# A third gate_up program and experts in an order made on the chip, in a hybrid decoder layer

## The chip, the cores and the metric

One NeuronCore of a Trainium2 chip runs the whole layer in one launch. The metric is the device time of one execution in microseconds (us). The kernel before has a median of 2191.45 us over 3 runs (2190.69 to 2195.38). The profiled execution took 2190.32 us.

## The reference

```python
# one layer: x (1, 1024, 1024) float32, 1024 tokens t of width D = 1024
h = rmsnorm(x)
p = h @ w_in                      # D x 3584: ret_q|ret_k|ret_v|ret_gate|sb_q|sb_k|sb_v
A = swish_gate(rmsnorm(retention(rotary(q), rotary(k), v)))   # 4 heads x 128
B = stick_breaking(rmsnorm(q), rmsnorm(k), v)                 # 8 heads x 64, strictly causal
x = x + concat(A, B) @ w_out
xn = rmsnorm(x)
top4 of xn @ w_router + b_router over 32 experts, softmax over the four
for each expert e, its tokens:
    gu = xn @ w_gate_up[e] + b_gate_up[e]          # 1024 x 2048, gate and up interleaved
    hidden = (clip(up) + 1) * min(gate, 7) * sigmoid(1.702 * gate)
    y = hidden @ w_down[e] + b_down[e]             # 1024 x 1024
x = x + sum over the four experts of weight * y
```

All inputs and the output are float32. How many tokens an expert gets is known on the chip only; 4096 pairs fall on 32 experts.

## The kernel before, in words

**Projection** (`project`, L946 and L953, until some 385 us). The product with `w_in` runs in two halves of 512 tokens. Operands are split in an upper part (rounded to fp32r) and a lower one (the rest), and three products add up: `products`. Tokens come to feature-major form by `turn_tile`: ScalarE takes sums of squares, VectorE inverts, and `x_norm` is made for tile 0 and 1 on one engine and for tiles 2 and 3 on POOL (L592), which then makes `w_lo[0]` (L594). `upper_tokens` (ScalarE) and `lower_tokens` (VectorE, L1337) split the tokens; for the second half both stand at group `NG // 2`, when the last group of the first half has left. Retention steps and the head norms are woven between the groups.

**Stick-breaking attention** (`scores`, `turn_rest`, `values`; some 385 to 508 us). `values` (L1069) multiplies by `dv`, differences of neighbouring rows of v. SyncE copies v shifted by one row into `dv` in two parts and POOL subtracts (L613), all of it after the last projection group.

**Output projection and router** (L1103 to L1133, until some 620 us). Each token tile goes through `out_proj`, `turn`, `route` and `route_sum` on TensorE, `residual`, `scaled`, `inverse_norm` and `best` (the four best logits) on VectorE; `route_sum` and `best` trail three tiles behind. `keep_busy` issues transposes nobody reads.

**Lists and tables** (some 620 to 647 us). Counts and ranks come from products with triangular ones (`f_rank`). `first_hot` and `token_list` make the index list of expert 0, POOL gathers its rows by indirect DMA, `turn_main` and `turn_over` transpose them. VectorE's `tables()` (L1620 to L1632) then makes what later experts need: three bf16 parts of each token's weight (`twx`) and the places of each token (`f_n`). It stands before block 0, and the engines' waits for it end just ahead of the first gate_up.

**The 32 expert blocks** (647 to some 2171 us). Each engine has a loop over the experts in their own order, n = 0 to 31: `block_pe` on TensorE, `block_dve` on VectorE, `block_act` on ScalarE, `load_expert` on SyncE. A block holds up to CAP = 168 tokens; further ones would go to a second loop of `more` blocks, which here runs zero times. In a block:

- TensorE loads the expert's count from `it_i` into a register (L1277) and chooses one of two gate_up programs by it (L1284): 140 tokens wide, or 168. Each has its own instructions. `gate_up` takes 8 steps f, each two parts of 8 matmuls with 128x128 float32 weights out of `gu_ring` (every second column) and `xT` as what moves (L1246). A float32 matmul is two instructions. After f = 3 `token_list` (24 small matmuls, L1162) makes the list of the next expert.
- `down` takes 48 matmuls of 512 columns (L1226), with the transposes of the next expert's tokens (L1169, L1175) in the middle, and for tokens over 128 64 narrow matmuls for each 32 rows (L1234, `down_over`), under a branch each.
- VectorE in each step f empties the bank (L1739, L1741), makes the hidden values (L1747, L1749) and their lower part (L1728), splits down weights (`lower`, L1723) and, after f = 1, compares positions for the next list (`list_hot`, L1644). The banks alternate, so TensorE's step f needs VectorE's emptying of step f - 2. In block 0 `table_part(f)` adds small operations for the table of further blocks.
- SyncE reloads `gu_ring` in four chunks of 2 MB and `dn_ring` in two as they come free.

The choice of the program, in block_pe:

```python
tokens = e.value_load(it_i[0:1, 1, bass.ds(n, 1)], min_val=-S, max_val=S)
...
    with e.If(tokens <= widths[half - 1]):
        choose(widths[:half])
    with e.Else():
        choose(widths[half:])
```

Of the kernel before, what the change touches and what calls it, by code (L numbers as in the profile page):

```python
# [60 lines left out]
WIDTHS = (140, CAP)  # L61
IT_STEPS = 17
F_SPREAD = 20
# [55 lines left out]
def layer(nc, x, attn_norm_g, w_in, ret_norm_g, sb_q_norm_g, sb_k_norm_g, w_out, ffn_norm_g,  # L119
          w_router, b_router, w_gate_up, b_gate_up, w_down, b_down, consts, rope, out):  # L120
    with ExitStack() as ctx:
# [81 lines left out]
        dv = region(ring, 3072, NT, CH)  # L203
# [44 lines left out]
        a_norm_p = sem("a_norm_p")  # L248
# [55 lines left out]
        e_norm = sem("e_norm")  # L304
        e_st = [sem(f"e_st{i}") for i in range(2)]
# [10 lines left out]
        it_step = sem("it_step")  # L316
        l_wrap = sem("l_wrap")
# [170 lines left out]
        f_w0 = region(work, 1576, NT, 4)  # L488
        f_t0 = region(work, 1608, NT)
        f_cnt = region(mix, 7744, NE)  # L490
        f_over = region(mix, 7776, NE)
# [4 lines left out]
        b_rows = region(work, 4096, 2048)[0:NE]  # L496
# [3 lines left out]
        dn_ring = region(ring, 16384, KD, D)  # L500

# [13 lines left out]
        def wait_norm(e, i):  # L515
            if 2 <= i < HT:
                e.wait_ge(a_norm_p, i - 1)
            else:
                e.wait_ge(a_norm, i + 1 if i < 2 else i - 1)

        @block.sync
        def _(sp_eng):
# [25 lines left out]
            for q in range(2):  # L548
                lo, n = HT * q, HT - 1 + q
                for r0, r1 in ((1, 113), (113, P)):  # L550
                    e.dma_start(dv[r0:r1, lo:lo + HT], sv[r0 - 1:r1 - 1, lo:lo + HT]).then_inc(z_shift[q], 16)
                e.dma_start(dv[0:1, lo + 1 - q:lo + HT], sv[P - 1:P, lo - q:lo + HT - 1]).then_inc(z_shift[q], 16)
# [3 lines left out]
            for c in range(2):  # L556
                e.dma_start(dn_ring[:, :, c * 512:(c + 1) * 512], dn_r[0, c]).then_inc(dn_in[c], 16)
            for i in range(NT):
                e.wait_ge(e_x2, 2 * i + 2)
                e.dma_start(outr[i], x2[:, i % 2]).then_inc(e_st[i % 2], 16)  # L560
                e.wait_ge(e_norm, i + 1)
                e.dma_start(xnr[i], xn2[:, i % 2]).then_inc(e_st[i % 2], 16)
            e.wait_ge(e_prj, 2 * NT)
            for c in range(4):
# [3 lines left out]
                e.dma_start(gu_ring[:, :, c * 512:(c + 1) * 512], gu_r[0, c]).then_inc(gu_in[c], 16)  # L568

# [8 lines left out]
            with e.Fori(1, NE) as n:  # L578
                load_expert(n, n)
# [8 lines left out]
        def _(e):  # L588
            for i in range(2, HT):
                e.wait_ge(a_inv, i + 1)  # L590
                e.wait_ge(a_tr, 2 * i - 2)
                e.tensor_scalar(x_norm[i % 2], x_in[i % HT], rstd[:, i:i + 1], None, ALU.mult).then_inc(a_norm_p, 1)  # L592
# [3 lines left out]
            e.dma_start(wr, w_router[0].rearrange("(k p) n -> p k n", p=P)).then_inc(rt_in, 16)  # L596
            for th in range(2):
                for q in range(2 * RH):
                    dst = (rqT if q < RH else rkT)[:, q % RH, :]
                    e.wait_ge(prj_free, freed(NG // 2 * th + q + 1))  # L600
                    e.tensor_tensor(dst, dst, prj_tmp[:, q % 2], ALU.add).then_inc(rope_ok, 1)
                for c in range(HT * th, HT * (th + 1)):
# [6 lines left out]
            e.memset(dv[0:1, 0], 0.0).then_inc(z_zero, 1)  # L609
            e.wait_ge(z_zero, 1)  # L610
            for i in range(NT):
                e.wait_ge(z_shift[i // HT], 48)
                e.tensor_tensor(dv[:, i], sv[:, i], dv[:, i], ALU.subtract).then_inc(z_dv, 1)  # L613
# [15 lines left out]
            e.wait_ge(e_st[1], 128)  # L629
# [8 lines left out]
            e.wait_ge(g_xT, 4)  # L638
# [40 lines left out]
        def _(e):  # L679
# [25 lines left out]
            def upper_tokens(th):  # L705
                e.wait_ge(a_hx, NT * (th + 1))
                if th:
                    e.wait_ge(prj, NG // 2)
                for k in range(0, KD, 2):
# [8 lines left out]
            root(HT - 1)  # L718
            upper_slab(0)
            upper_tokens(0)  # L720
            for g, u in enumerate(groups):
                th, c = u["th"], u["c"]
                if g == NG // 2:
                    upper_tokens(1)
# [27 lines left out]
                if g in SPLIT:  # L752
                    upper_slab(SPLIT[g])
                if g in NORM:
# [72 lines left out]
            for i in range(NT):  # L827
# [7 lines left out]
                e.activation(e_dump, x2[:, i % 2], ACT.Square, accum_out=ssq2[:, i:i + 1]).then_inc(e_sq, 1)  # L835
                e.wait_ge(e_ms, i + 1)
# [5 lines left out]
            for i in range(NT - 3, NT):  # L842
# [3 lines left out]

            e.wait_ge(e_log, NT)
            e.wait_ge(e_st[0], 128)
            e.wait_ge(e_st[1], 128)
            e.dma_start(b_rows, b_gate_up[0]).then_inc(bias_in, 16)  # L850
# [6 lines left out]
            e.wait_ge(sc_done, 48)  # L857
            e.wait_ge(f_step, F_SPREAD)
            e.activation(bias_d, b_raw, ACT.Copy).then_inc(b_cast, 1)
            for g in range(1, 3):  # L860
                e.wait_ge(b_sub, g)
                for h in range(g, 3):
                    rows = slice(h * NE, (h + 1) * NE)
                    cp = e.activation(bias_d[rows], b_raw[rows], ACT.Copy)
                cp.then_inc(b_cast, 1)
# [19 lines left out]
            def block_act(n):  # L885
                for f in range(KD):
# [8 lines left out]
                    e.activation(hid_hi[:, f], hid[:, f, 0:P], ACT.Copy).then_inc(h_hi, 1)  # L895
                for q in range(5, 8):
# [911 lines left out]
```

## Time and profile before

| | |
|---|---|
| median of 3 runs | 2191.45 us (2190.69 to 2195.38) |
| profiled execution | 2190.32 us, span 2188.0 us |
| mean granted TensorE clock | 0.988 |
| TensorE matmuls busy | 2126.4 us, 97% of the span |
| TensorE weight loads busy | 1891.9 us, 86% (beside the matmuls) |
| VectorE | 1271.9 us, 58% |
| ScalarE | 765.9 us, 35% |
| GpSimd (POOL) | 346.5 us, 16% |
| DMA | 509.53 MB, mean 233 GB/s |
| the chain that ended last | PE 95%, DVE 2%, issue 1%, DMA 1% |

The span runs from the first to the last instruction; the execution's own time has 2.3 us around it. PE is TensorE's matmuls, PEld its weight loads, DVE VectorE, ACT ScalarE, SP SyncE; a q behind an engine is its sequencer. "issue" is time in which an engine waited for nothing that the profile shows. A clock of 1.00 is the full 2.4 GHz, 0.5 the lower level. The chain names at each moment what the end of the run hung on, so its shares, not the busy times, say where time can be taken out.

### The profile page before, as it was taken

Reading aid. Unit: us, or ns where it says so; the run is one execution under the profiler, and the core shown is the slowest. Engines: PE = TensorE matmul, PEld = TensorE weight load, DVE = VectorE, ACT = ScalarE, POOL = GpSimd, SP = SyncE. Lnnn points to the kernel's source line nnn. Section 1 sums busy time; section 2 is a strip of 40 time slices with the busy share of each in tenths; the row PEclk is TensorE's granted clock in tenths of the full one; section 3 lists DMA queues with packets and bytes.
Section 4 is the critical chain, followed back from the end, with each engine's and each line's share of the span. In section 5 each row is a group of like instructions: output and inputs, shape, how many; then the busy total and the mean of one; then the engine's idle time right before and its main releaser. Section 6 shows DMA issues by size and latency. Waiting matters only on the chain.

```text
span 2188.0 us, 41248 instructions
## 1 busy us (share of the span) xinstructions
PE 2126.4 (97%) x16059; PEld 1891.9 (86%) x16060; DVE 1271.9 (58%) x2564; ACT 765.9 (35%) x1369; POOL 346.5 (16%) x243
## 2 busy tenths in 40 slices
PE   7999999899979999999999999999999999999996
PEld 6887888677868999898899999899999999999996
DVE  6434534886466665456556655555666655666654
ACT  4143133666222333233333323333333332333332
POOL 3100200200011111111121111111212111212121
PEclk9999999999979999999999999999999999999998
DMA  5321221304366988788789888877998887999883
GB/s 179 105 79 58 97 96 39 116 1 154 126 209 220 323 307 293 238 279 307 274 298 318 306 293 280 307 270 263 320 325 307 306 294 264 319 327 331 309 290 89
DMA packets 253683, 509.53 MB, mean 233 GB/s; under 512 B 7466, under 2 KB 36318, under 8 KB 253342
## 3 DMA queue, kind: packets, MB, share of 16 engines
q1 hardware_dynamic: 230124, 451.95, 57.9%
q0 software_dynamic: 21968, 51.67, 9.6%
q10 hardware_dynamic: 1536, 5.15, 0.7%
q8 instruction: 38, 0.62, 0.1%
q14 instruction: 17, 0.14, 0.0%
HBM read 473.09 MB, written 33.55 MB: 232 GB/s over the span
## 4 chain that ended last, share of the span: by engine, by line
PE 95%; DVE 2%; issue 1%; DMA 1%; POOL 0%; ACT 0%; ACTq 0%; SPq 0%; DVEq 0%; POOLq 0%
PE bank L1246 46%; PE bank L1226 16%; PE bank L946 10%; PE bank L953 4%; PE bank L1234 3%; PE bank L1056 2%; PE bank L1069 2%; PE bank L1103 1%; PE bank L1169 1%; PE bank L1105 1%; PE bank L1104 1%; PE bank L1162 1%; PE bank L1040 1%; PE bank L1175 1%; PE bank L1211 1%
## 5 line engine op out<-in xcount | busy, mean ns | idle before, releaser
L1246 PE MATMUL bank<-hx,ring 128*128 128x140 f32 (+1 forms) x8192 | 1021.9, 287 | 7.5 <-DVEq L1684 7.5
L1246 PEld LDWEIGHTS bank<-hx,ring 128*128 128x128 f32 x8192 | 1015.1, 197 | 10.3 <-DVEq L1684 7.7
L1226 PE MATMUL bank<-work_r,hx_r 128*128 128x512 f32 x1024 | 335.0, 408 | 0.0
L1723 DVE TENSOR_TENSOR mix_r<-ring,work_r 128x1024 fp32r<-128x1024 f32 x256 | 305.0, 1223 | 41.1 <-ACT work_r L872 40.9
L889 ACT ACTIVATE hx<-hx 128x168 f32<-128x168 f32 x256 | 88.0, 344 | 595.8 <-DVE hx L1739 593.4
L1739 DVE TENSOR_SCALAR hx<-bank,small 128x168 f32<-128x168 f32 x256 | 100.3, 392 | 298.7 <-PE bank L1246 289.3
L872 ACT ACTIVATE work_r<-ring 128x1024 fp32r<-128x1024 f32 x256 | 257.7, 1042 | 0.0
L1226 PEld LDWEIGHTS bank<-work_r,hx_r 128*128 128x128 f32 x1024 | 188.1, 189 | 43.9 <-issue 10.4
L1226 PE MATMUL bank<-mix_r,hx_r 128*128 128x512 f32 x512 | 200.0, 391 | 0.0
L649 POOL DMA_INDIRECT out_x<-hx,small x32 | 52.0, 1625 | 659.7 <-ACT hx L882 621.3
L880 ACT ACTIVATE hx<-bank,small 128x512 f32<-128x512 f32 x64 | 44.0, 688 | 313.9 <-PE bank L1175 167.3
L616 POOL DMA_INDIRECT hx<-xn_scratch,small x33 | 33.9, 1028 | 574.1 <-issue 568.1
L895 ACT ACTIVATE hx_r<-hx 128x128 fp32r<-128x128 f32 x256 | 78.8, 308 | 109.0 <-DVE hx L1749 109.0
L946 PE MATMUL bank<-hx_r,mix_r 128*128 128x512 f32 x480 | 112.5, 392 | 3.6 <-DVE hx_r L1337 3.6
L1226 PEld LDWEIGHTS bank<-mix_r,hx_r 128*128 128x128 f32 x512 | 96.1, 188 | 21.0
L946 PE MATMUL bank<-hx_r,work_r 128*128 128x512 f32 x480 | 113.7, 394 | 0.0
L946 PEld LDWEIGHTS bank<-hx_r,mix_r 128*128 128x128 f32 x480 | 89.6, 188 | 23.5 <-issue 5.2
L1644 DVE TENSOR_TENSOR work<-hx,cst 128x3072 bf16<-128x3072 f32 x32 | 107.2, 3351 | 0.0
L946 PEld LDWEIGHTS bank<-hx_r,work_r 128*128 128x128 f32 x480 | 89.7, 188 | 20.2 <-issue 1.9
L652 POOL DMA_INDIRECT out_x<-hx,small x64 | 100.7, 1573 | 19.5 <-issue 19.5
L1741 DVE TENSOR_SCALAR hx<-bank,small 128x168 f32<-128x168 f32 x256 | 98.0, 383 | 0.0
L1658 DVE TENSOR_TENSOR hx<-bank,small 128x512 f32<-128x512 f32 x66 | 42.6, 686 | 86.0 <-PE bank L1169 86.0
(244 smaller groups left out, 2318.4 us busy)
## 6 DMA issues: line engine op xcount, KB each, us to landing
ring<-in_w_gate_up SPq DMA_DIRECT2D x128, 2048.0 KB, 11.0
ring<-in_w_down SPq DMA_DIRECT2D x64, 2048.0 KB, 17.5
mix<-in_w_in SPq DMA_DIRECT2D x14, 1024.0 KB, 5.0
work<-in_w_in SPq DMA_DIRECT2D x14, 1024.0 KB, 5.1
ring<-in_x SPq DMA_DIRECT2D x8, 512.0 KB, 6.3
hx<-in_w_out SPq DMA_DIRECT2D x1, 4096.0 KB, 14.0
work<-in_x ACTq DMA_DIRECT2D x8, 512.0 KB, 4.7
out_x<-work SPq DMA_DIRECT2D x8, 512.0 KB, 4.5
```

The source lines that it names most:

```text
L652: e.indirect_dma_start(out=out_quarters, in_=y_o[:, r], in_offset=None, compute_op=ALU.add, out_offset=bass.IndirectOffsetOnAxis(ap=idx_sc ...
L872: e.activation(dn_hi[:, nh, k:k + 2], dn_ring[:, k:k + 2, nh * CH:(nh + 1) * CH], ACT.Copy).then_inc(c_hi, 1)
L889: e.activation(sg[:, f % 2], g1[:, f % 2], ACT.Sigmoid, scale=GALPHA).then_inc(m_sig, 1)
L895: e.activation(hid_hi[:, f], hid[:, f, 0:P], ACT.Copy).then_inc(h_hi, 1)
L946: mm = e.matmul(dst, ws[b][:, k, u["s"] * P:(u["s"] + 1) * P], xs[:, k, :], start=k == 0 and (xs is x_hi and ws is w_hi), stop=k == KD - 1 ...
L953: mm = e.matmul(dst, xs[:, KD // 2 * b + k, u["s"] * P:(u["s"] + 1) * P], ws[b].rearrange("p (k a) n -> p k (a n)", a=2)[:, k, :], start=b ...
L1226: mm = e.matmul(bank[2 + t][:, :], h[:, k], w[:, t, k], start=False, stop=k == KD - 1 and w is dn_lo, skip_group_check=True)
L1246: mm = e.matmul(bank[f % 2][:, part * CAP:part * CAP + w], gu_ring[:, k, f * 256 + part:(f + 1) * 256:2], xT[:, k, 0:w], start=k == 0, sto ...
L1644: e.tensor_tensor(hot, pos_s.unsqueeze(2).to_broadcast([P, NT, NH * P]), slot_at.unsqueeze(1).to_broadcast([P, NT, NH * P]), ALU.is_equal) ...
L1723: e.tensor_tensor(dn_lo[:, nh, k:k + 2], dn_ring[:, k:k + 2, nh * CH:(nh + 1) * CH], dn_hi[:, nh, k:k + 2].bitcast(F32), ALU.subtract).the ...
L1739: e.tensor_scalar(g1[:, b], bank[b][:, 0:CAP], be[:, f:f + 1], GLIM, ALU.add, ALU.min)\
L1741: e.tensor_scalar(u1[:, b], bank[b][:, CAP:2 * CAP], be[:, 8 + f:9 + f], GLIM + 1.0, ALU.add, ALU.min).then_inc(m_up, 1)
```

## The change

- `WIDTHS` has three widths, 128, 140 and 168, so `block_pe` has three gate_up programs, in this order in the code, and down behind them. The second loop (`more`) has the three as well.
- Blocks 0, 1 and 2 stay experts 0, 1 and 2 (`FIXED`). While block 1 runs, VectorE's `order_part` gives every later expert a key (its class by count: to 128, to 140, over; then its number), ranks the keys by 32x32 comparisons, and writes experts and counts in that order into `it_i`. `it_go` then opens blocks 3 to 31 for TensorE and SyncE. SyncE and VectorE load each block's expert from `it_i`.
- `tables()` no longer stands before block 0. `second_lists` (expert 1's list alone) and `weight_table`, `second_hot`, `place_table` run on VectorE inside block 0, `table_part` in block 2. The bias parts of POOL and ScalarE go into block 0.
- Openings: at the start `x_norm` of tile 2 is made on ScalarE and of tile 3 on VectorE, with 14 filler transposes ahead of the first tile; half of the second half's token splits come three groups earlier; the first four tiles of `dv` are shifted and subtracted during the projection; 20 filler transposes stand before the output projection; `route_sum` and `best` of the first tiles come earlier, and the last normalised tile is stored from ScalarE's queue; `b_gate_up` is loaded early into a part of `dn_ring`, whose second half is loaded later; the bias transposes come right behind the counts.

The diff, cut (a "..." marks what is left out):

```diff
-WIDTHS = (140, CAP)
-IT_STEPS = 17
-F_SPREAD = 20
+WIDTHS = (128, 140, CAP)
+LATER = (128, 140)
+FIXED = 3
+IT_STEPS = 29
+F_SPREAD = 21
...
+            def shifted(q):
+                lo = HT * q
+                for r0, r1 in ((1, 113), (113, P)):
+                    e.dma_start(dv[q][r0:r1], sv[r0 - 1:r1 - 1, lo:lo + HT]).then_inc(z_shift[q], 16)
+                e.dma_start(dv[q][0:1, 1 - q:HT], sv[P - 1:P, lo - q:lo + HT - 1]).then_inc(z_shift[q], 16)
...
+                if j == NSLAB // 2 + 4:
+                    e.wait_ge(prj_free, freed(NG // 2))
+                    e.wait_ge(xs_lo, KD)
+                    shifted(0)
...
-            for c in range(2):
-                e.dma_start(dn_ring[:, :, c * 512:(c + 1) * 512], dn_r[0, c]).then_inc(dn_in[c], 16)
+            e.dma_start(dn_ring[:, :, 0:512], dn_r[0, 0]).then_inc(dn_in[0], 16)
+            e.dma_start(b_rows, b_gate_up[0].rearrange("e (a n) -> e a n", n=512)).then_inc(bias_in, 16)
...
+            e.wait_ge(bias_tr, 1)
+            e.dma_start(dn_ring[:, :, 512:1024], dn_r[0, 1]).then_inc(dn_in[1], 16)
...
             with e.Fori(1, NE) as n:
-                load_expert(n, n)
+                e.wait_ge(it_go, n + 1)
+                load_expert(n, e.value_load(it_i[0:1, 0, bass.ds(n, 1)], min_val=0, max_val=NE - 1))
...
-            for i in range(2, HT):
-                e.wait_ge(a_inv, i + 1)
-                e.wait_ge(a_tr, 2 * i - 2)
-                e.tensor_scalar(x_norm[i % 2], x_in[i % HT], rstd[:, i:i + 1], None, ALU.mult).then_inc(a_norm_p, 1)
...
+            e.activation(x_norm[0], x_in[2], ACT.Copy, scale=rstd[:, 2:3]).then_inc(a_norm_2, 1)
...
+                if g == NG // 2 - 3:
+                    upper_tokens(1, 0, KD // 2)
...
+                if i == NT - 1:
+                    logits_part(NT - 3)
...
+            e.dma_start(xnr[NT - 1], xn2[:, (NT - 1) % 2]).then_inc(e_last, 16)
...
             e.wait_ge(const_in, 16)
+            keep_busy(14, bank[2])
...
+            keep_busy(20, bank[4])
...
+                    if nh and i >= 3:
+                        route_sum(i - 3)
...
-            keep_busy(10, bank[4])
+
+            e.wait_ge(bias_in, 16)
+            e.wait_ge(e_x2, 16)
+            for j in range(16):
+                mm = e.transpose(bank[j // 8][:, (j % 8) * NE:(j % 8 + 1) * NE],
+                                 b_rows[:, j % 8 // 2, j % 2 * 256 + j // 8:j % 2 * 256 + 256:2], cst[0:NE, C_ID:C_ID + NE])
+            mm.then_inc(bias_tr, 1)
...
-            keep_busy(8, bank[3])
+            keep_busy(4, bank[3])
...
             with e.Fori(0, NE) as n:
+                e.wait_ge(it_go, n + 1)
                 block_pe(n)
...
+            to_raw(0)
+            normalise(3)
+            for i in range(1, HT):
...
+                if 3 <= i < NT:
+                    best(i - 3)
...
+            def second_lists():
+                step(e.tensor_scalar(pos_t, tok_id, f_cnt[:, 1:2], None, ALU.add))
+                step(e.scalar_tensor_tensor(pos_t, rank[:, :, 1], -2.0, pos_t, ALU.mult, ALU.add))
+                step(e.tensor_tensor(pos_t, pos_t, f_n[:, :, 1], ALU.mult))
+                step(e.tensor_tensor(pos_s, rank[:, :, 1], pos_t, ALU.add))
+                step(weight_parts(1))
+                step(e.tensor_reduce(f_t, f_b.rearrange("p i k e -> p i e k"), X, ALU.add))
+
+            def second_hot():
+                e.tensor_tensor(hot, pos_s.unsqueeze(2).to_broadcast([P, NT, NH * P]),
+                                slot_at.unsqueeze(1).to_broadcast([P, NT, NH * P]), ALU.is_equal).then_inc(l_hot, 1)
+                e.sem_inc(l_wrap, 1)
+                e.sem_inc(l_pos, 1)
+
+            def weight_table():
                 step(e.tensor_copy(twx[:, :, 0:NE, 0], f_t))
                 step(e.tensor_tensor(f_t, f_t, twx[:, :, 0:NE, 0], ALU.subtract))
                 step(e.tensor_copy(twx[:, :, 0:NE, 1], f_t))
                 step(e.tensor_tensor(f_t, f_t, twx[:, :, 0:NE, 1], ALU.subtract))
                 step(e.tensor_copy(twx[:, :, 0:NE, 2], f_t))
                 step(e.memset(twx[:, :, NE, :], 0.0))
+
+            def place_table():
+                e.memset(it_base, 0.0)
+                e.memset(it_low, 0.0)
...
-            tables()
...
+            def order_part(f):
+                if f == 0:
+                    table(e.tensor_copy(c_f, it_i[:, 1, 0:NE]))
+                    table(e.tensor_scalar(c_class, c_f, float(LATER[0]), None, ALU.is_gt))
+                    for w in LATER[1:]:
+                        table(e.scalar_tensor_tensor(c_class, c_f, float(w), c_class, ALU.is_gt, ALU.add))
+                    table(e.scalar_tensor_tensor(c_class, iota_e, float(FIXED), c_class, ALU.is_ge, ALU.mult))
+                    table(e.scalar_tensor_tensor(c_key, c_class, float(NE), iota_e, ALU.mult, ALU.add))
+                elif f == 2:
+                    table(e.tensor_tensor(c_less, c_key.unsqueeze(2).to_broadcast(square),
+                                          c_key.unsqueeze(1).to_broadcast(square), ALU.is_gt))
+                    table(e.tensor_reduce(c_rank, c_less, X, ALU.add))
+                elif f == 3:
+                    table(e.tensor_tensor(c_at, iota_e.unsqueeze(2).to_broadcast(square),
+                                          c_rank.unsqueeze(1).to_broadcast(square), ALU.is_equal))
+                elif f == 4:
+                    table(e.tensor_tensor(c_less, c_at, iota_e.unsqueeze(1).to_broadcast(square), ALU.mult))
+                    table(e.tensor_reduce(it_f[:, 0, 0:NE], c_less, X, ALU.add))
+                elif f == 5:
+                    table(e.tensor_tensor(c_less, c_at, c_f.unsqueeze(1).to_broadcast(square), ALU.mult))
+                elif f == 6:
+                    table(e.tensor_reduce(it_f[:, 1, 0:NE], c_less, X, ALU.add))
+                    table(e.tensor_copy(it_i[:, :, FIXED:NE], it_f[:, :, FIXED:NE]))
+                    e.sem_inc(it_go, NE - FIXED)
...
-                    if f == 1:
+                    if f == 1 and opening:
+                        second_hot()
+                    elif f == 1:
                         e.wait_ge(l_sum, n + 1)
                         if x_next is None:
-                            x_next = e.value_load(it_i[0:1, 0, bass.ds(n + 1, 1)], min_val=0, max_val=NE)
+                            x_next = e.value_load(it_i[0:1, 0, n + 1:n + 2] if isinstance(n, int) else
+                                                  it_i[0:1, 0, bass.ds(n + 1, 1)], min_val=0, max_val=NE)
                         list_hot(n + 1, x_next)
-                    if opening:
+                    if opening and f == 0:
+                        weight_table()
+                    if opening and f == 2:
+                        place_table()
+                    if ordering:
+                        order_part(f)
+                    if tabling:
                         table_part(f)
...
-            block_dve(0, 0, 1, True)
-            assert built[0] == IT_STEPS
-            with e.Fori(1, NE - 1) as n:
-                block_dve(n, n, n + 1)
-            block_dve(NE - 1, NE - 1)
+            block_dve(0, 0, 1, opening=True)
+            block_dve(1, 1, 2, ordering=True)
+            block_dve(2, 2, tabling=True)
+            assert built[0] == IT_STEPS, built[0]
+            with e.Fori(FIXED, NE) as n:
+                block_dve(n, e.value_load(it_i[0:1, 0, bass.ds(n, 1)], min_val=0, max_val=NE - 1))
```

TensorE, the expert loop. Before, the block's register load, the 140 program and the start of the 168 program, as the instructions stand (`bank<-hx,ring` are the gate_up products):

```order
L1277 TENSOR_LOAD hx
L1277 ISA x2
L1284 COMPARE_AND_BRANCH
L1239 ISA
L1242 ISA
L1243 ISA
L1246 MATMUL bank<-hx,ring 128x140 x16
...
L1284 UNCONDITIONAL_BRANCH
L1239 ISA
L1242 ISA
L1243 ISA
L1246 MATMUL bank<-hx,ring 128x168 x16
```

After, the same place: the first branch leads over the 128 program to a second one.

```order
L1313 TENSOR_LOAD hx
L1313 ISA x2
L1320 COMPARE_AND_BRANCH
...
L1282 MATMUL bank<-hx,ring 128x128 x16
...
L1320 UNCONDITIONAL_BRANCH
L1320 COMPARE_AND_BRANCH
...
L1282 MATMUL bank<-hx,ring 128x140 x16
...
L1320 UNCONDITIONAL_BRANCH
...
L1282 MATMUL bank<-hx,ring 128x168 x16
...
L1322 UNCONDITIONAL_BRANCH
L1247 MATMUL bank<-cst,small 128x512
```

Each program holds 128 such matmuls and the 24 of `token_list`; `down` begins at L1247, behind all three.

VectorE, block 1 after the change (emptying a bank is L1830, the list L1709, the sort L1785 to L1802):

```order
L1709 TENSOR_TENSOR work<-hx,cst 128x3072
L1830 TENSOR_SCALAR hx<-bank,small 128x168
L1832 TENSOR_SCALAR hx<-bank,small 128x168
L1817 TENSOR_TENSOR hx_r<-hx,hx_r 128x128
L1838 TENSOR_TENSOR hx<-hx 128x168
L1840 SCALAR_TENSOR_TENSOR hx<-hx 128x168
L1792 TENSOR_TENSOR mix<-small 128x1024
L1794 TENSOR_REDUCE small<-mix 128x32
...
L1796 TENSOR_TENSOR mix<-cst,small 128x1024
L1812 TENSOR_TENSOR mix_r<-ring,work_r 128x1024 x2
```

The operations of the sort (over 1024 elements each) stand between the steps, ahead of the next emptying.

## Rows read from the trace of the kernel before

**Rows 1.** The page's chain that ended last, shares of the span by line.

```profile
PE bank L1246 46%; PE bank L1226 16%; PE bank L946 10%; PE bank L953 4%; PE bank L1234 3%; PE bank L1056 2%; PE bank L1069 2%; PE bank L1103 1%; PE bank L1169 1%; PE bank L1105 1%; PE bank L1104 1%; PE bank L1162 1%; PE bank L1040 1%; PE bank L1175 1%; PE bank L1211 1%
```

**Rows 2.** Chain by time (start us, us, what); 841: a 168-wide block, 1573: at most 128 tokens.

```profile
841.27 18.24 PE bank L1246 x128
...
1573.57 15.26 PE bank L1246 x128
...
1618.01 7.03 PE bank L1246 x59
```

**Rows 3.** Groups by form: xcount | busy us, mean ns | idle before <-releaser, whole run.

```profile
L1246 PE MATMUL bank<-hx,ring 128*128 128x140 f32 x6912 | 837.4, 283 | 7.5 <-DVEq L1684 7.5
...
L1246 PE MATMUL bank<-hx,ring 128*128 128x168 f32 x1280 | 184.5, 306 | 0.0
...
L1234 PE MATMUL bank<-ring,hx 128*32 128x256 f32 x1216 | 68.8, 379 | 0.0
```

**Rows 4.** Timeline of TensorE, 140 to 144 us: start us, us, operation.

```profile
140.37 1.05 PE L985 MATMUL bank<-ring,work 128*128 128x128 f32 x8
...
142.16 1.06 PE L1004 MATMUL bank<-ring 128*128 128x128 f32 x8
```

**Rows 5.** Windows: us, busy us (x) of PE, PEld, DVE, ACT, POOL, PEclk, DMA share, GB/s.

```profile
1573.57:1588.83 15.26, 15.26 (x135) 15.24 (x135) 8.59 (x20) 4.66 (x10) 4.78 (x3) 1.00 0.95 282
1589.41:1604.77 15.36, 15.36 (x130) 15.34 (x130) 12.35 (x30) 6.85 (x13) 3.63 (x3) 1.00 1.05 393
392.80:399.70 6.90, 6.05 (x31) 4.34 (x32) 3.15 (x3) 1.49 (x5) 6.90 (x6) 0.51 0.91 316
```

**Rows 6.** Chain by time, block 0.

```profile
647.24 17.93 PE bank L1246 x128
...
665.75 15.37 PE bank L1246 x128
681.12 2.79 issue
```

**Rows 7.** Branches of L1284 (all; after 700 us) and L1298: xcount: ns min/median/max.

```profile
L1284 PEldq COMPARE_BRANCH  x59: 76/169/4927, 638.0 to 2155.8; - x59
...
L1284 PEldq COMPARE_BRANCH  x57: 76/169/209, 700.2 to 2155.8; - x57
...
L1298 PEldq COMPARE_BRANCH  x1: 3287/3287/3287, 2169.2 to 2169.2; - x1
```

**Rows 8.** VectorE operation on 1024 elements: xcount: ns min/median/max, first and last start.

```profile
L1612 DVE TENSOR_TENSOR work<-cst,work x1: 1226/1226/1226, 631.0 to 631.0; 128x1024 f32<-128x1024 bf16 x1
```

**Rows 9.** The index load L1277 of two blocks, and those blocks' first matmuls in the chain.

```profile
L1277 PEldq TENSOR_LOAD <-hx x1: 303/303/303, 1042.4 to 1042.4; - x1
1044.89 15.26 PE bank L1246 x128
...
L1277 PEldq TENSOR_LOAD <-hx x1: 303/303/303, 1279.5 to 1279.5; - x1
1281.03 1.99 PE bank L1246 x14
```

**Rows 10.** Waits around the openings (us in total, times, longest), and POOL's group L592.

```profile
PE bank L946 <- DVE hx_r L1337: 2.6, 1, 2.6
...
PE bank L1069 <- POOL ring L613: 4.1, 1, 4.1
...
PE bank L1103 <- DVE hx_r L1548: 3.4, 1, 3.4
...
L592 POOL TENSOR_SCALAR ring<-ring,small 128x1024 f32<-128x1024 f32 x2 | 5.7, 2842 | 10.4 <-PE bank L918 10.4
```

**Rows 11.** DMA queues, 675 to 705 us and 740 to 2160 us: packets, MB, share.

```profile
q8 instruction: 5, 0.08, 1.1%
...
q1 hardware_dynamic: 183383, 369.78, 72.6%
q0 software_dynamic: 20160, 47.20, 13.5%
```

More of the change, by code:

```diff
@@ L316, in layer @@
         it_step = sem("it_step")
+        it_go = sem("it_go")
         l_wrap = sem("l_wrap")
@@ L596, in _, with differences @@
             e.dma_start(wr, w_router[0].rearrange("(k p) n -> p k n", p=P)).then_inc(rt_in, 16)
+            def differences(q):
+                for i in range(HT):
+                    e.wait_ge(z_shift[q], 48)
+                    e.tensor_tensor(dv[q][:, i], sv[:, HT * q + i], dv[q][:, i], ALU.subtract).then_inc(z_dv, 1)
             for th in range(2):
@@ L608, in _ @@
             e.wait_ge(prj_free, freed(NG))
[L609 to L613, printed above, removed]
+            differences(1)
             def gather_main(landed):
@@ L703, in upper_slab, with upper_tokens @@
                 e.activation(w_hi[j % 2], w_raw[j % 2], ACT.Copy).then_inc(ws_hi, 1)
-            def upper_tokens(th):
+            def upper_tokens(th, first, last):
                 e.wait_ge(a_hx, NT * (th + 1))
                 if th:
-                    e.wait_ge(prj, NG // 2)
-                for k in range(0, KD, 2):
+                    e.wait_ge(prj, end_of[NSLAB // 2 - 2] if first == 0 else NG // 2)
+                for k in range(first, last, 2):
                     e.activation(x_hi[:, k:k + 2], x_raw[:, k:k + 2], ACT.Copy).then_inc(xs_hi, 1)
@@ L855, in _, with bias_part @@
                 .then_inc(bias_ok, 1)
[L857 to L865, printed above, removed]
+            def bias_part(g):
+                if g == 0:
+                    e.wait_ge(sc_done, 48)
+                    e.wait_ge(f_step, F_SPREAD)
+                    e.activation(bias_d, b_raw, ACT.Copy).then_inc(b_cast, 1)
+                else:
+                    e.wait_ge(b_sub, g)
+                    for h in range(g, 3):
+                        rows = slice(h * NE, (h + 1) * NE)
+                        cp = e.activation(bias_d[rows], b_raw[rows], ACT.Copy)
+                    cp.then_inc(b_cast, 1)
             def upper(n, q):
@@ L1089, in _, with route_sum @@
             e.wait_ge(rt_in, 32)
+            def route_sum(i):
+                e.wait_ge(e_pev, i + 1)
+                if i:
+                    e.wait_ge(e_logb, 6 * i - 5)
+                e.matmul(bank[7][:, 0:NE], l_part[:, i % 2], cst[:, C_SEL:C_SEL + NE], start=True, stop=True).then_inc(e_log, 1)
             def out_proj(i):
@@ L1127, in route @@
                 mm.then_inc(e_part, 1)
-            def route_sum(i):
-                e.wait_ge(e_pev, i + 1)
-                if i:
-                    e.wait_ge(e_logb, 6 * i - 5)
-                e.matmul(bank[7][:, 0:NE], l_part[:, i % 2], cst[:, C_SEL:C_SEL + NE], start=True, stop=True).then_inc(e_log, 1)
             for i in range(NT + 3):
@@ L1189, in _ @@
             mm.then_inc(p_list, 1)
-            e.wait_ge(bias_in, 16)
-            e.wait_ge(e_x2, 16)
-            for j in range(16):
-                mm = e.transpose(bank[j // 8][:, (j % 8) * NE:(j % 8 + 1) * NE],
-                                 b_rows[:, (j % 8) * 256 + j // 8:(j % 8) * 256 + 256:2], cst[0:NE, C_ID:C_ID + NE])
-            mm.then_inc(bias_tr, 1)
+            keep_busy(10, bank[4])
             e.wait_ge(l_hot, 1)
@@ L1332, in lower_slab, with lower_tokens @@
                 e.tensor_tensor(w_lo[j % 2], w_raw[j % 2], w_hi[j % 2].bitcast(F32), ALU.subtract).then_inc(ws_lo, 1)
-            def lower_tokens(th):
-                for q in range(KD // 2):
+            def lower_tokens(th, first, last):
+                for q in range(first // 2, last // 2):
                     e.wait_ge(xs_hi, KD // 2 * th + q + 1)
```

112 lines of the change are left out of this document (63 added, 49 removed).

## The prediction

> **What bounds the kernel now.** I read the chain of waits first. TensorE carries it: the gate_up line L1246 alone is 46% of the span and the down line L1226 16% [rows 1]. So a term counts only where TensorE gets shorter work or stops waiting, and a wait on any other engine costs nothing until TensorE stands for it. The chain inside an expert block of the loop (the stretch of an expert with at most 128 tokens) has no gap: 15.26 us for 128 instructions of L1246, TensorE busy for all of the other half's 15.36 [rows 5], and the next block's first matmul 44.44 us after this one's [rows 2]. The groups by form give 6912 instructions at a moving width of 140 and 1280 at 168, 256 to a block: 27 and 5 blocks [rows 3]. L1234, the rows over 128, ran 1216 times at 64 for up to 32 rows: 19 pieces [rows 3]; one block has two of them, so 18 experts hold over 128 tokens, 5 of them over 140, and **14 hold at most 128**. Those 14 are computed 140 wide today.
>
> **The 128-wide program.** 128 instructions take 15.26 us at width 140 and 18.24 at 168 [rows 2], so 119.2 and 142.5 ns each: 0.83 ns per column and 2.5 ns besides. At 128 columns this gives 109.2. The weight load of 128 columns runs beside each matmul and may set a floor. Other f32 matmuls with 128 columns show one: 16 of them, eight each of L985 and L992, start between 140.37 and 142.16 us, 111.9 ns each [rows 4]. L1246 reads its weights with a stride of two, which rows 4 do not test, so its floor may lie anywhere up to the 119.2 it runs at. Per block of 256 the gain is 256 x (119.2 - 109.2) = 2.6 us at best, 1.9 at 111.9, 1.1 halfway from there to no gain (115.0), 0 at 119.2. I take 1.9: it is the nearest row, and at 140 and 168 one line per column still fits with 2.5 ns over. 14 x 1.9 = **-27** (-36 to -15, and 0 as a rival).
>
> Do the weights arrive in time? In this half block the DMA engines are 0.95 busy [rows 5]. That is the one resource near its limit, and a shorter block pulls 12 MB through 42.5 us instead of 44.4. If it saturates, the loss is a part of the 27 and not a cost beyond it: I count nothing. VectorE works 8.59 us in the first half and 12.35 in the second [rows 5]; two halves of 14.3 still hold that.
>
> **The tables.** `tables()` stands between the last token copies and the first gate_up; L1246's only idle time is 7.5 us behind it [rows 3]. It moves to block 0, where VectorE waits for TensorE's slow first steps. The first half of block 0 took 17.93 us against 15.37 for its second [rows 6]: the clock had fallen to its lower level (1.2 GHz) in the wait, and a shorter wait may give back 1 of these 2.6. -7.5 - 1. What takes it back: block 0 is expert 0, of the 140 class (its half takes 15.37 and a piece of L1234 follows), so it must now jump over the 128 program, and a jump over a program that has not run is dear. The one in block 0 today took 4927 ns, and TensorE stood 2.79 us for it [rows 6, 7]. The new one comes at the entry, where little is queued: **+3** (0 to 5). The old exit jump stays as it is. Sum **-5.5** (-9 to -2).
>
> **The sort.** `order_part` adds, in block 1, six compare, multiply or reduce steps over 32x32 = 1024 elements with one more reduce, 1.23 us each by L1612's operation of that size [rows 8], so some 8.6 us, of which 8.4 fall in steps 2 to 6. The gate_up part of a block holds 20.9 us of VectorE work [rows 5], steps 1 to 6 some 19.2 of it, since step 0 has only a step's 1.7; with the sort 27.6. In the time from the end of its step 1 to that of step 6 TensorE has five steps of 3.6 us and the token list, 18.6, and VectorE may be one to two steps late (5.4 in the middle) before a PSUM bank is missing. 27.6 - 18.6 - 5.4 = 3.6, and the last hidden parts reach the down product about 1 us late: **+4.5** (0 to +8). Block 2's `table_part` is what block 0 has today, without a stall: 0. The waits on `it_go` in TensorE's and SyncE's streams hold the loop only at block 3; SyncE's queue behind it has the weight loads of expert 3, which can't start before the ring is free anyway, late in block 2's gate_up: 0. The index load per block on VectorE and SyncE is a register load of about 0.3 us (TensorE's own takes that [rows 9]), and VectorE is busy only 8.59 of the first half's 15.26 us: 0.
>
> **The openings.** Each shortens one wait, and each is bounded by it. At the start, two normalisations leave POOL (2842 ns each, with w_lo0 queued behind [rows 10]) for ScalarE and VectorE: -4 (0 to -5). At the half boundary TensorE waited 2.6 us for x_lo; half of it is now made before: -2. At the attention's start it waited 4.1 us for POOL's differences [rows 10], behind a DMA that now runs during the projection for the first four tiles: -4, and the lower clock in the 6.9 us after it (0.51 [rows 5]) should partly go: -2. At out_proj keep_busy can only keep the clock, the 3.4 us wait [rows 10] stays: -1.7. Router tail: one `best` and two logits less behind the last tile: -1.6. Bias transposes moved off the chain and four fewer filler transposes: -2.5. Sum -17.8; each moved step meets the next late thing (SyncE's queue now waits for x_lo before w_in slabs; the last xn store sits on ScalarE's queue), so I give a fifth back: **-14** (-20 to -6).
>
> **Switches of class.** Sorted, the classes run 140, 128, 140, then 128, 140, 168 in blocks: four jumps into a program that lies elsewhere, at 0 to 4 us each: **+3** (0 to +17). Here the classes' own new code is fetched.
>
> Sum: -27 - 5.5 + 4.5 - 14 + 3 = **-39** against the profiled execution's 2190.3, so 2151.3; the median of the runs shown is 1.1 us above that execution, so **2152**. Own range 2137 to 2172.
>
> **Rival 1, slower: the loop no longer stays loaded.** Today instructions arrive by their own DMA queue: 5 packets of 16 KB between 675 and 705 us, and from 740 to 2160 us none at all [rows 11]. So the whole loop stays loaded. Counted in the program, one turn of the loop is some 1,560 TensorE instructions (512 matmuls and weight loads in each gate_up program, 48 of the token list), with the third program about 2,130; at 64 bytes each 6.1 packets become 8.3. The trace shows the seven packets held over which today's loop lies, and says nothing of a ninth. If eight are held, the loop's last piece pushes out its first, and the jump back misses once per block. A miss is 3287 ns (L1298, idle queues) to 4927 (L1284, full ones) [rows 7]. The index load leads the block's first matmul by 2.5 us (1042.4 to 1044.89) and after a block with rows over 128 by 1.5 [rows 9]; some 1 us of it is register and branch work, so 1.5 and 0.5 are cover. 14 x (1.8 to 3.4) + 17 x (2.8 to 4.4) = 73 to 123 us, less 39: **2225 to 2275**. It decides from the point where the loop exceeds what is held. Sorting does not help the jump back. For it: the 4927 ns jump, and 16 KB packets fetched only once the code is near. Against: no jump after 700 us took over 209 ns [rows 7], so nothing is dropped as long as it fits.
>
> The Trainium skill ("Runtime: NRT & Kernel Launch", section "Instruction fetch mechanics") gives TensorE room for 2048 instructions, refilled 256 at a time, and makes a taken branch outside the window wait for its page; by that figure this rival holds. The same section speaks of a window of two pages, by which today's loop would stall every block, and the trace shows that it doesn't.
>
> **Rival 2: the weight load is the floor.** If L1246 can't go below 119 ns, the 27 are gone and the rest stays: -12, **2179**. The 111.9 ns of rows 4 speaks against it.
>
> **Rival 3: the change does not do what it says**, as the sort comes too late or in the old order: then TensorE waits on `it_go` at block 3 once, at most 5 us, and the classes are mixed. With the loop resident this is 2157, inside the first case.
>
> **How the numbers follow.** A measurement of this kernel tells about 0.2% (4.4 us) from no change. The first case with rival 3: 0.57. Rival 1: 0.38. Rival 2: 0.05. Faster 0.59 (the first case and most of the second rival), slower 0.37, same 0.04, where a cheap rival 1 meets the gains. The range must reach from 2137 into the middle of rival 1: 2137 to 2262.
>
> **What would show it.** In the profile after: L1246 at form 128x128 x3584 with halves near 14.3 us; the chain without gaps at the block borders; no packets of the instruction queue from 800 us on. One packet or more per block there, and an "issue" gap of 2 to 4 us before each block's first L1246, prove rival 1. The gap before the first L1246 should be near 0, block 1 should hold 3 to 6 us of waits on VectorE, and the waits of rows 10 should be gone save that at out_proj. If the blocks of 128 shrink by under 1 us, rival 2 holds.

## The result, and the profile after

The changed kernel takes **2581.3 us** (median of 4 runs, 2578.2 to 2584.5); beside it the kernel before took 2192.1. The ratio is 1.177 (95% interval 1.175 to 1.180): 389 us slower, where 39 us faster were forecast, and far above the range. The page of the kernel after begins (busy us, share of the span, instructions), with its instruction queue, the chain by engine and the gate_up group:

```profile
PE 2202.0 (85%) x16089; PEld 1946.5 (76%) x16090; DVE 1281.5 (50%) x2583; ACT 726.9 (28%) x1339; POOL 343.2 (13%) x241
...
q8 instruction: 210, 3.44, 0.6%
...
PE 79%; issue 11%; DVE 6%; ACT 1%; DMA 1%; ACTq 0%; POOL 0%; DVEq 0%; POOLq 0%
...
L1282 PE MATMUL bank<-hx,ring 128*128 128x128 f32 (+2 forms) x8192 | 1055.6, 293 | 211.7 <-issue 210.3
```

TensorE has about as much to do as before, but it stands 210 us on "issue" just ahead of gate_up matmuls, that is, it waits for nothing that the profile shows. The queue that brings instructions moved 210 packets of 16 KB, where before it moved 38. In the DMA view, which answers to [rows 11], the queues are, for 862 to 1388 us (twelve blocks of the 128 class) and for 1527 to 1600 us (one block of the 140 class):

```profile
q1 hardware_dynamic: 74873, 150.99, 79.7%
q0 software_dynamic: 8064, 18.88, 14.6%
...
q8 instruction: 10, 0.16, 0.9%
```

There is no instruction packet at all in the twelve blocks, and there are ten in one block of the next class. The branches of TensorE agree, since a dear branch (one of over 1 us) stands only where packets come; the lines are L1320 (the choice of the program) and L1330 (the jump back), first for 860 to 1380 us, then for one block of the 140 class and the edges of its neighbours (count: ns min/median/max):

```profile
L1320 PEldq COMPARE_BRANCH  x23: 76/169/169, 889.2 to 1374.3; - x23
L1330 PEldq COMPARE_BRANCH  x11: 207/208/208, 901.9 to 1342.9; - x11
...
L1320 PEldq COMPARE_BRANCH  x3: 81/6326/7522, 1527.6 to 1567.8; - x3
L1330 PEldq COMPARE_BRANCH  x2: 4051/4074/4096, 1522.6 to 1595.9; - x2
```

In the first stretch no branch is dear, though the loop is one of 2,130 instructions there too and each block jumps over two programs. In the second the jump over the 128 program takes 7.5 us, the jump over the 168 program 6.3 and the jump back 4.1. In the chain by time (start us, us, what) that block reads:

```profile
1524.51 11.16 issue
1535.67 18.49 PE bank L1282 x128
...
1554.75 15.38 PE bank L1282 x128
...
1576.57 3.23 issue
1579.80 7.01 PE bank L1262 x24
...
1597.87 10.45 issue
```

The windows of its parts (columns as in [rows 5]) show what the gaps cost besides:

```profile
1524.50:1535.70 11.20, 0.04 (x2) 0.04 (x1) 0.33 (x2) 1.42 (x3) 4.78 (x3) 0.66 0.89 258
1535.67:1554.16 18.49, 18.49 (x135) 18.47 (x136) 8.28 (x18) 1.65 (x5) 0.00 (x0) 0.83 0.69 231
1554.75:1570.13 15.38, 15.37 (x128) 15.16 (x128) 12.34 (x30) 6.84 (x13) 3.71 (x3) 1.00 0.79 283
1570.13:1579.80 9.67, 0.61 (x1) 0.39 (x2) 5.34 (x9) 3.49 (x5) 0.00 (x0) 0.62 0.82 287
```

From one block's gap to the next are 73.4 us, where such a block took 47.9: 11.2 us of gap ahead of gate_up, 9.7 ahead of down, 3.2 in the first half, whose mean granted clock is 0.83 after 0.66 in the gap (18.49 us against 15.26 in [rows 2]), and 1.5 in the first down products (7.01 us in the chain against 5.47 without a gap). Over the 11 sorted blocks of this class that is 281 us, over the five of the 168 class about 100, over blocks 0 and 2 another 28.

The groups by form answer to [rows 3]. Behind them stands the chain: the entry of block 0, the first matmuls of blocks 1 and 2, and the second halves of two blocks of the 128 class:

```profile
L1282 PE MATMUL bank<-hx,ring 128*128 128x128 f32 x3584 | 431.1, 283 | 8.4 <-issue 7.2 <-DVE hx L1832 1.2
L1282 PE MATMUL bank<-hx,ring 128*128 128x140 f32 x3328 | 428.7, 294 | 113.3 <-issue 113.0 <-DVE hx L1832 0.2
L1282 PE MATMUL bank<-hx,ring 128*128 128x168 f32 x1280 | 195.9, 318 | 90.0 <-issue 90.0
```

```profile
627.63 1.97 PE bank L1210 x8
...
631.81 5.61 issue
637.42 9.47 PE bank L1282 x64
...
702.41 9.19 PE bank L1282 x64
...
750.29 7.64 PE bank L1282 x64
...
876.33 15.18 PE bank L1282 x128
...
920.43 15.18 PE bank L1282 x128
```

The 14 blocks are 128 wide as intended, but half a block takes 15.18 us against 15.37, and the block 44.10 against 44.44.

### The profile page after: what moved, and what is told of

It reads as the page before. It is cut to its first block, busy times and chain, and to the rows that moved or that the text cites. A ratio compares the mean times of both kernels' runs of the same rounds, so it can differ in the third digit from the quotient of the medians.

```text
span 2576.3 us, 41675 instructions
## 1 busy us (share of the span) xinstructions
PE 2202.0 (85%) x16089; PEld 1946.5 (76%) x16090; DVE 1281.5 (50%) x2583; ACT 726.9 (28%) x1339; POOL 343.2 (13%) x241
## 4 chain that ended last, share of the span: by engine, by line
PE 79%; issue 11%; DVE 6%; ACT 1%; DMA 1%; ACTq 0%; POOL 0%; DVEq 0%; POOLq 0%
PE bank L1282 38%; PE bank L1262 15%; PE bank L978 8%; PE bank L985 3%; PE bank L1270 3%; DVE mix_r L1812 2%; PE bank L1088 1%; PE bank L1101 1%; PE bank L1144 1%; PE bank L1210 1%; PE bank L1146 1%; PE bank L1145 1%; ACT work_r L900 1%; PE bank L1203 1%; PE bank L1072 1%
## 5 line engine op out<-in xcount | busy, mean ns | idle before, releaser
L1282 PE MATMUL bank<-hx,ring 128*128 128x128 f32 (+2 forms) x8192 | 1055.6, 293 | 211.7 <-issue 210.3
L1282 PEld LDWEIGHTS bank<-hx,ring 128*128 128x128 f32 x8192 | 1045.4, 202 | 220.9 <-issue 217.9
L1262 PE MATMUL bank<-work_r,hx_r 128*128 128x512 f32 x1024 | 355.8, 430 | 69.2 <-issue 63.5
L1830 DVE TENSOR_SCALAR hx<-bank,small 128x168 f32<-128x168 f32 x256 | 100.2, 391 | 516.4 <-PE bank L1282 502.1
L1262 PEld LDWEIGHTS bank<-work_r,hx_r 128*128 128x128 f32 x1024 | 202.7, 203 | 120.5 <-issue 80.4
L1262 PE MATMUL bank<-mix_r,hx_r 128*128 128x512 f32 x512 | 211.0, 412 | 0.0
L1262 PEld LDWEIGHTS bank<-mix_r,hx_r 128*128 128x128 f32 x512 | 103.4, 202 | 24.4
L1709 DVE TENSOR_TENSOR work<-hx,cst 128x3072 bf16<-128x3072 f32 x31 | 103.9, 3352 | 0.0
```

Source lines behind the costliest of these rows:

```text
L1262: mm = e.matmul(bank[2 + t][:, :], h[:, k], w[:, t, k], start=False, stop=k == KD - 1 and w is dn_lo, skip_group_check=True)
L1282: mm = e.matmul(bank[f % 2][:, part * CAP:part * CAP + w], gu_ring[:, k, f * 256 + part:(f + 1) * 256:2], xT[:, k, 0:w], start=k == 0, sto ...
L1709: e.tensor_tensor(hot, pos_s.unsqueeze(2).to_broadcast([P, NT, NH * P]), slot_at.unsqueeze(1).to_broadcast([P, NT, NH * P]), ALU.is_equal) ...
L1830: e.tensor_scalar(g1[:, b], bank[b][:, 0:CAP], be[:, f:f + 1], GLIM, ALU.add, ALU.min)\
```

## The theory, and a count made with it

**Theory 1.** TensorE's instructions lie in pieces of 256 (16 KB). Eight are held; a landing in a piece also calls the next one; the one brought or used longest ago goes first. A block touches, in the order of the code, the head of the loop, its own gate_up program and down, with one piece ahead behind each. For the 128 class these are eight pieces: head and program adjoin (four, with the one ahead), then down (four). For the 140 class, whose program lies in the middle, they are ten; for the 168 class too, as it lands at the second branch behind the 128 program on its way. Eight pieces just fit. Ten pieces in turn through eight places means that each is gone when it is wanted.

These rules make a small count (the pieces' positions from the fetches of the two traces), which says how many fetches and dear branches each block has. For the changed kernel it gives 0 where one block of the 128 class follows another, 10 where blocks of the other two follow each other, 51 dear branches in all; the trace has 0, 140 packets in the 14 such blocks between the first and the last of that stretch, and 51 (without the one behind the loop). As the positions come from this trace, the agreement is a fit; the runs below are the test.

My first count had seven pieces for the 128 class, and the expectation of e1 says so. The packets show eight. In the DMA view, block 3 (128 class, behind one of 140; 810.4 to 857.7 us) has the first line, and block 16 (140 class, behind one of 128; 1387.5 to 1448.5 us) the second:

```profile
q8 instruction: 4, 0.07, 0.6%
...
q8 instruction: 6, 0.10, 0.7%
```

With seven pieces they would be 3 and 7; with eight they are the 4 and 6 that came.

**Rivals:** the sort, its index loads and waits; any loop over 2048 instructions; the length of the way that is jumped over.

## The experiments

**e1, the 128 program alone taken out.**

```diff
-WIDTHS = (128, 140, CAP)
-LATER = (128, 140)
+WIDTHS = (140, CAP)
+LATER = (140,)
-IT_STEPS = 29
+IT_STEPS = 28
```

> The changed kernel without its 128-wide program (classes to 140 and over; the sort, the moved tables and the openings stay). Theory 1 (TensorE holds eight pieces of 256 instructions, each jump or step also calls the next one, the oldest goes first; a block of the 140 or 168 class touches nine or ten of the three-program loop, one of the 128 class seven): the loop of 1,565 instructions lies in seven pieces and one ahead, nothing is fetched after block 1, no branch over 0.4 us after it, time 2192 less some 7 for the openings, 8 for the tables, plus 4 for the sort, = 2178 to 2184. Rival (the sort, the index loads or the wait on it_go make the blocks long): over 2400, with blocks of the 140 class near 74 us.

2175.4 us (2175.2 to 2177.7), ratio 0.992 (0.990 to 0.994). 38 packets, as before, on its page:

```profile
q8 instruction: 38, 0.62, 0.1%
```

Everything else of the change is in this kernel, so in this setting the 389 us and 17 more are the third program's. Without it, the sort, the index loads and the wait on it_go cost next to nothing.

**e2, and without the sort** (order_part reduced to the copy of the counts and the opening of it_go).

> As the run before, and the experts stay in their own order (order_part only copies the counts and opens it_go). Theory 1: no fetches in the loop either, block 1 shorter by the 3.8 us that it is longer than the other blocks of its class in the changed kernel: 2174 to 2180. If sorting gives something back through fewer changes of program, it is not faster than the sorted one.

2176.8 us (2173.6 to 2181.2), ratio 0.993 (0.991 to 0.995). Block 1 is shorter (44.56 us against 46.40 in e1), though by 1.8 and not by 3.8 us, and the two kernels' times can't be told apart: the sort is nearly free, and with two programs buys nothing.

**e3, the choice turned.** The 168 class jumps from the loop's head.

```diff
-                    half = len(widths) // 2
+                    half = (len(widths) + 1) // 2
```

> The changed kernel with the choice turned: the first branch asks for 140, so a block of the 168 class jumps from the head of the loop straight to its program and no longer lands at a second branch behind the 128 program. Theory 1: the 168 class now touches seven or eight pieces (28, 29, 33 to 37 in my count) and stays loaded: its blocks fall from 74 us to 54 (fetches from 10 a block to 0, after the first), the 140 class stays at 73 to 74 with 10 fetches: 2581 less 80 to 100 = 2480 to 2500. Rival (any loop over 2048 instructions misses once the far part is used; or the gap of 18 us is the length of the way jumped over, some 3.7 us per piece): the 168 class stays at 74 us, 2581.

2484.7 us (ratio 1.133), 97 less than the changed kernel. The chain has the halves of two blocks of the 168 class without a gap between blocks, 53.90 us from one to the next:

```profile
2253.34 18.24 PE bank L1282 x128
2272.17 18.35 PE bank L1282 x128
2307.24 18.24 PE bank L1282 x128
```

The first block of the 168 class fetches two pieces, the other four none. The blocks of the 140 class stay at 72 to 75 us with 10 fetches each. The loop is as long as before, the way jumped over too; only one landing on the way is gone. That refutes both the bare length and the distance.

**e4, three programs in the kernel before, experts in their own order.**

```diff
-WIDTHS = (140, CAP)
+WIDTHS = (128, 140, CAP)
```

> The kernel before with WIDTHS (128, 140, 168) and nothing else: three programs, the experts' own order. Theory 1: a block that follows one of the same class can find its pieces only if the class is the 128 one; my count gives some 47 dear branches (51 in the changed kernel) at about 7.9 us each (2581 less 2177, over 51): 2192 + 371 less 5 = 2540 to 2570. Rival (the sort is what costs): near 2190.

2493.2 us (ratio 1.137). The count of dear branches was right: 47 in the loop (214 packets in all), none where a 128 block follows another, one at a change into or out of that class, three in a 140 or 168 block behind one of those two. The fetches are 0, 4 to 6 and 9 to 11, where the count with eight pieces has 0, 4 to 6 and 9 or 10. My price was too high (2493 less 2187 over 47 is 6.5 us instead of 7.9). The sorted kernel has about as many dear branches (51) and is still 88 us slower than this one; e9 asks where that comes from.

**e5 and e6, code that never runs.** The two-program kernel of e2, with transposes under a branch that is never taken at the start of down, 128 of them in e5 and 64 in e6:

```diff
             def down(n, tokens):
+                with e.If(tokens > S - 1):
+                    keep_busy(128, bank[4])
```

> The two-program kernel in the experts' own order (e2_two_natural, 2177 us), with 128 filler transposes (256 instructions) at the start of the down part under a branch that is never taken: they never run, and the loop has 1,821 instructions, under 2048. Theory 1: what counts are pieces of 256, with the one called ahead at each landing; in my count every block now touches nine pieces where eight are held: 8 or 9 fetches and 2 dear branches in nearly every block, 286 fetches in all, each block 15 to 20 us longer: 2177 + 31 x 18 = 2650 to 2800. (If the loop's head lies a quarter of a piece later than I think, only the five blocks of the 168 class and their followers: 51 fetches, some 2220.) Rival (2048 instructions of any alignment are held): 2177 to 2190, 38 or 39 fetches.

2728.5 us (ratio 1.244), 318 packets, 9 in nearly every block (my count had 8 and 9 by turns, 286 in all), 90 dear branches in the loop, nearly three a block where I had counted two (why the third one is dear stays open):

```profile
q8 instruction: 318, 5.21, 0.9%
```

> The same with 64 filler transposes (128 instructions). Theory 1: eight pieces still hold a block of either class: no fetches after block 1, 2177 to 2185 (one more branch per block, some 0.2 us of sequencer time that lies behind queued work). Rival (the branch or filler itself costs): as far above 2177 as the run before in half measure.

2180.2 us (ratio 0.994), 38 packets. A loop of 1,821 instructions is refetched in every block and one of 1,693 is not, though the 128 more never run. This fits a limit of eight pieces, the called-ahead ones among them, and not one of 2048 instructions of any position.

**e7, the stride of the weights.** The kernel before with widths 128 and 168, and gate_up's weights read as neighbouring columns, so that gate and up are computed from other columns than the reference's:

```diff
-WIDTHS = (140, CAP)
+WIDTHS = (128, CAP)
-                                          gu_ring[:, k, f * 256 + part:(f + 1) * 256:2], xT[:, k, 0:w],
+                                          gu_ring[:, k, f * 256 + part * P:f * 256 + (part + 1) * P], xT[:, k, 0:w],
```

> The kernel before with widths 128 and 168, and the gate_up weights read as 128 neighbouring columns instead of every second one (other columns are multiplied, so gate and up hold other features; the amount of work is the same). Of 128 instructions at width 128, half a block: 15.18 us in the changed kernel (118.6 ns each). Theory A (the stride of the weight load sets that floor): 14.2 to 14.4 us, 111 to 112.5 ns, as L985 to L1004 run, and the load's record falls from 196 to 191 ns. Rival B (a floor of its own for these f32 passes, or of VectorE's steps): 15.1 to 15.2 as before.

2240.6 us in its one run, as 18 experts are now computed 168 wide. Half a block at width 128 in its chain, and all its weight loads by form:

```profile
721.53 14.40 PE bank L1246 x128
```

```profile
L1246 PEld LDWEIGHTS bank<-hx,ring 128*128 128x128 f32 x8192 | 1064.1, 191 | 10.6 <-DVEq L1684 7.7
```

112.5 ns each instead of 118.6, with the same weights brought in. The stride sets the floor, and it holds 1.6 of the 1.9 us a block that I had counted on.

**e8, the tables back before block 0** (second_lists, weight_table and place_table called there, not in block 0), the rest as e2.

> e2_two_natural with the list, weight and place tables made again before block 0 instead of inside it. Theory 1 (the wait of 7.5 us before the first gate_up is real time and block 0 hides the tables): 2177 + 6 to 9 = 2183 to 2186. Rival (block 0 pays for them with waits on VectorE): 2177 within 2.

2183.5 us (2183.2 to 2187.0), ratio 0.996 (0.995 to 0.998). The old wait is back, as the page shows:

```profile
L1282 PE MATMUL bank<-hx,ring 128*128 128x140 f32 (+1 forms) x8192 | 1021.9, 287 | 8.4 <-DVEq L1751 8.0
```

So moving the tables gives 6.7 us. The rest, this kernel against the one before, is 9.3: the openings, less 2 us that block 2 now takes longer (49.9 us against 47.9), since `table_part` stands in it.

**e9, the loop a quarter of a piece further on**, the changed kernel with 40 filler transposes in place of 8 behind turn_over.

> The changed kernel with 32 more filler transposes (64 instructions, 3.5 us if they are not covered) in TensorE's stream ahead of the loop, so that the whole loop lies a quarter of a piece further on. Theory 1 with the pieces where I place them: today the jump out of the 140 program lands on the last few instructions of a piece (34.97 of 35), so two pieces must come one after the other before down can run, and TensorE stands 9.7 us there; with the shift it lands at 35.2, one piece is enough, 9 fetches instead of 10 in a block of the 140 class, and the block falls from 73.5 to about 68.5 (where the three-program kernel in its own order has them); the 128 class stays without fetches at 44.1. Eleven blocks: 2581 - 55 + 3 = 2520 to 2540. Rival (the pieces do not matter, only the length): 2581 to 2585.

2507.0 us (ratio 1.143), 74 less than the changed kernel, and 13 below what I expected. In the DMA view a block of the 140 class has nine packets:

```profile
q8 instruction: 9, 0.15, 1.0%
```

Its chain ahead of down:

```profile
1544.26 4.35 issue
1548.61 0.61 PE bank L1247
1549.22 7.47 PE bank L1262 x24
```

The gap ahead of down is 4.4 us instead of 9.7, the block 66 to 67 us instead of 73.4. The same program with the same jumps thus loses or saves 74 us by where its loop begins. The gap ahead of down fits a landing on the last instructions of a piece, which has to wait for two pieces. In e4, whose loop begins elsewhere, that gap is 4.5 us too (at 1252.85), so this accounts for most of the 88 us between the changed kernel and e4. Four more dear branches at 6.5 us would be another 26, an estimate; against that stand the 16 us that e4 lacks of the tables and openings.

## Why the prediction was wrong

**The step that failed** is the one that the sum took for granted: that the loop stays loaded, which I gave 0.57. The rows spoke neither way beyond seven packets, and I let the better story (a gain in each term) have the larger half. I had the right rival, with the right number of places, and **mis-stepped in its mechanics**: "the jump back misses once per block" and "Sorting does not help the jump back". A block of the 128 class behind another misses never, one of the other two in a row of such blocks at all three of its jumps. What counts is how many pieces one block touches, with those called ahead, and not whether the loop's end pushes out its head. The rival's 73 to 123 us came out near 400 (281, 100 and 28), partly by that number and partly because I priced a miss by its branch alone. Right behind one dear jump, the next took 6.5 to 7.6 us, as the piece called ahead by the first was still on its way (the order of the packets suggests this, no run tests it), and the half block behind each such gap ran at a lower granted clock (3.2 us).

The row was there for a better bound: 5 packets came in block 0 for one jump over an unrun program [rows 11], and the jump cost 4.9 us [rows 7]. Had I written down the pieces of each class in turn, as I did afterwards, the three dear jumps of the 140 class would have stood against eight places.

The Trainium skill ("Runtime: NRT & Kernel Launch", section "Instruction fetch mechanics") gives room for 2048 instructions in blocks of 256, sequential prefetch, and a stall for a taken branch outside the window. The runs agree with the blocks, the prefetch and eight of them (e5 against e6); the two-page window in the same section they contradict, since twelve blocks jump over two programs without a fetch.

**The other terms**, of which the first missed by 22 us and the others by 2 to 5:

| term | forecast | measured |
|---|---|---|
| 128-wide program, 14 blocks | -27 | -5 (0.34 us each; 118.6 ns a matmul instruction) |
| tables moved | -8.5 | -6.7 (e8 against e2) |
| new jump into block 0's program | +3 | +5.6 (issue at 631.81) |
| the sort, block 1 | +4.5 | +1.8 (46.40 in e1 against 44.56 in e2) |
| `table_part` in block 2 | 0 | +2.0 (49.9 against 47.9) |
| openings | -14 | -9.3 (e8 against before, with the 2.0 in it) |

The first is rival 2 in nearly full strength, to which I gave 0.05. The +3 for the switches of class can't be read apart from the failed step: blocks 1, 2, 3 and 16 have 4 to 6 packets each. In the changed kernel block 1 is 3.8 us longer than a later one of its class (47.88 against 44.10), but block 3, which has no sort, is 1.8 longer too.

For the first term, I took the floor of matmuls with plain weights and noted that the stride was untested; e7 shows the stride to be just that difference. Of the openings, the half boundary gave nothing (the wait is 2.9 us instead of 2.6), and from the projection's end to the last product of the attention it is 121.5 us instead of 123.8, where I had counted 6.

## What to carry to other kernels

Before adding a variant of code to a loop, write down for each path the 256-instruction pieces it lands in, with the next one behind each landing, and compare with eight: paths of eight stayed loaded here (the 128 class, and the 168 class in e3), and paths of nine did not (e5, e9), at 18 to 26 us a block, where the variant's gain was 0.3 us. Code that never runs counts if it pushes the rest apart; a second branch on the way counts as a landing; the queue that carries instructions shows it, with packets or none per turn. And a pace measured with plain weights is no floor for strided ones. The best version here is the change without its third program (e1, 2175.4 us, 0.8% faster than before; e2, without the sort, can't be told from it).

## What the runs showed of the hardware

- By the packets and branches of six kernels (the changed one, e3, e4, e5, e6, e9), TensorE held eight pieces of 256 instructions; 128 instructions that never run made the difference between 38 and 318 packets (e6, e5).
- A jump to a piece that was not held took TensorE's sequencer 3.3 to 6.8 us (7.7 once in e4 and once in e7), and up to 7.9 right behind another such jump.
- Float32 matmul instructions with 128 moving columns: 118.6 ns with every second weight column, 112.5 with neighbouring ones (mean load records, over both widths, of 197 ns in the kernel before and 191 in e7).
- After a gap of 11 us (11.20) TensorE's mean granted clock over the next 18 us was 0.83.
